# Where a two-block transformer kernel does its modulation steps, frees its last ring blocks and ends its expert stages

## What is computed

```python
# first block, each of two layers
x = x + token_mixer(rms_norm(x, norm_mix[l]), w_in[l], ...)       # two attentions, gates, projections
x = x + peer_ffn(rms_norm(x, norm_ffn[l]), peer_query[l], ...)     # 8 heads x 16 experts of 16384
...
# peer_ffn, for a chunk of 128 tokens
sv, si = lax.top_k(s, PEER_TOPK)                                   # product keys, 2 x 128
act = gelu(einsum('td,thkd->thk', xc, expert_down[eidx]))
out = einsum('thk,thkd->td', g * act, expert_up[eidx])
...
# second block: every layer is modulated by a vector c (and a second stream by c_ctx)
mod = jnp.split(silu(c) @ w_mod[l] + b_mod[l], 6, axis=-1)
p = (rms_norm_2(x, g_norm1[l]) * (1 + scale1) + shift1) @ w_in[l]
x = mixers_and_ffn(x, p, attend_query_blocks(q, k, v), ...)        # attention, Fourier, convolution, pooling, SwiGLU
```

## Time and profile before

| | us |
|---|---|
| median of three runs | 2689.86 |
| lowest and highest | 2688.56, 2691.87 |
| the profiled execution | 2686.94 |
| its span | 2684.9 |
| TensorE matmuls busy | 2498.2 (93% of the span) |
| VectorE, ScalarE, GpSimd busy | 1472.8, 938.3, 595.5 |
| bytes moved by DMA | 817.47 MB, mean 304 GB/s |

### The profile page before, as it was taken

One profiled execution on the slowest core, in us unless ns is written; L12 is line 12 of the kernel. 1 busy time (PEld: TensorE's weight loads), 2 busy tenths in 40 slices (PEclk: granted clock), 3 DMA queues, 4 the chain that ended last, 5 costly groups with the idle time before them and its releaser, 6 DMA issues.

```text
span 2684.9 us, 29496 instructions
## 1 busy us (share of the span) xinstructions
PE 2498.2 (93%) x9800; PEld 1699.9 (63%) x9800; DVE 1472.8 (55%) x3162; ACT 938.3 (35%) x2317; POOL 595.5 (22%) x600
## 2 busy tenths in 40 slices
PE   7999998988888989998998889999889999999999
PEld 6668655533444546677555555567356888868888
DVE  3623576799877637414867776778647200172000
ACT  2351344445544323432444444432446100162000
POOL 0000233333444410001333333333413000030000
PEclk9999899999999999999999999999999999999999
DMA  6574999999999984667999999999972444424444
GB/s 244 176 284 167 370 426 427 427 392 413 404 427 427 420 356 141 250 235 282 413 427 426 427 427 411 421 426 423 423 304 79 148 150 157 159 93 141 148 150 157
DMA packets 113647, 817.47 MB, mean 304 GB/s; under 512 B 12432, under 2 KB 14528, under 8 KB 14944
## 3 DMA queue, kind: packets, MB, share of 16 engines
q0 software_dynamic: 75136, 549.29, 49.1%
q1 hardware_dynamic: 38368, 266.35, 26.8%
HBM read 814.54 MB, written 1.05 MB: 304 GB/s over the span
## 4 chain that ended last, share of the span: by engine, by line
PE 60%; DMA 21%; DVE 11%; issue 4%; ACT 3%; POOL 0%; ACTq 0%; DVEq 0%; SPq 0%; POOLq 0%
PE work L668 43%; DMA arena<-experts,arena 20%; PE acc L668 15%; DVE arena L2001 3%; DVE arena L1790 3%; PE work L760 1%; ACT L1467 1%; DVE small L1790 1%; DMA ring<-stream 1%; ACT arena L1477 1%; POOL arena L631 0%; ACT arena L1469 0%; DVE arena L2239 0%; DMA c<-consts 0%; DVE arena L1949 0%
## 5 line engine op out<-in xcount | busy, mean ns | idle before, releaser
L668 PE MATMUL acc<-arena 128*128 128x512 f32 (+1 forms) x1900 | 888.2, 616 | 124.0 <-ACT arena L1477 121.5
L668 PE MATMUL work<-arena,ring 128*128 128x256 f32 (+2 forms) x3524 | 768.0, 379 | 7.7 <-DMA ring<-stream 2.2
L668 PEld LDWEIGHTS work<-arena,ring 128*128 128x128 f32 x3524 | 667.5, 191 | 112.5 <-issue 17.6
L631 POOL DMA_INDIRECT arena<-experts,arena x512 | 532.3, 1040 | 901.1 <-PE acc L668 720.6
L668 PEld LDWEIGHTS acc<-arena 128*128 128x128 f32 (+1 forms) x1900 | 358.8, 196 | 556.2 <-issue 358.6
L2001 DVE SCALAR_TENSOR_TENSOR arena<-arena,h 128x1024 f32<-128x1024 f32 x256 | 311.9, 1226 | 172.5 <-DMA arena<-experts,arena 169.5
L2001 DVE SCALAR_TENSOR_TENSOR arena<-arena,acc 128x1024 f32<-128x1024 f32 x256 | 308.5, 1220 | 162.1 <-DMA arena<-experts,arena 148.8
L668 PE MATMUL work<-h,ring 128*128 128x256 f32 (+1 forms) x1440 | 329.4, 381 | 8.0 <-DMA ring<-stream 3.8
L668 PEld LDWEIGHTS work<-h,ring 128*128 128x128 f32 x1440 | 268.7, 193 | 76.3 <-issue 37.1
L1467 ACT ACTIVATE arena<-arena 128x2 f32<-128x2 f32 x256 | 52.0, 203 | 608.7 <-DVE arena L2001 404.8
L668 PE MATMUL work<-lent,ring 128*128 128x256 f32 x992 | 224.2, 379 | 0.0
(11 more groups left out here) (263 smaller groups left out, 1834.9 us busy)
## 6 DMA issues: line engine op xcount, KB each, us to landing
ring<-stream SPq DMA_DIRECT2D x252, 1024.0 KB, 5.2
arena<-experts,arena POOLq DMA_INDIRECT x512, 12.5
arena<-na_bias POOLq DMA_DIRECT2D x2, 2048.0 KB, 13.5
arena<-consts POOLq DMA_DIRECT2D x1, 2304.0 KB, 10.9
lent<-consts POOLq DMA_DIRECT2D x2, 1024.0 KB, 7.4
arena<-consts POOLq DMA_DIRECT2D x1, 1816.0 KB, 19.9
x<-x_in SPq DMA_DIRECT2D x1, 1024.0 KB, 5.5
xc<-ctx_in POOLq DMA_DIRECT2D x1, 1024.0 KB, 11.0
```

The source lines that it names most:

```text
L631: pool.indirect_dma_start(rows[:, m % ROWS, :], None, experts[l], bass.IndirectOffsetOnAxis(ap=expert[:, n:n + 1], axis=0))\
L668: ins = nc.tensor.matmul(o, w, r, start=start, stop=stop, **kw)
```

## The change

It moves and counts modulation steps anew, always 24 per layer. Before the norm's sum stand 0 steps in layer 0 and 3 in layer 1 (`MOD_FIRST`); after it 3 in both (1 and 3 before). In layer 1 the units 4, 8 and 12 of the attention have no step. Behind the attention and behind the branch projections stands one step each (2 and 2 before in layer 0, 1 and 1 in layer 1). Of the three steps at the query, one stands before the first score, one behind it and one before the second first-query pass; the first two stand ahead of the query's block in the stream. SP waits for the tokens before it issues the ring. The load of `lent` for layer 1 moves from the end of layer 0 to behind the first projection of layer 1. The four kept ring blocks are released by slots 251 to 254. The last group's two slots are weighed one by one, and the first half of the sums is released by its own semaphore. In layer 1 the last side sum comes before slot 252.

```diff
-MOD_NORM, MOD_TURN, MOD_MERGE, MOD_QUERY = (1, 3), (2, 1), (2, 1), 3
+MOD_FIRST, MOD_NORM = (0, 3), (3, 3)
+MOD_UNITS = [[u for u in range(N_GATE) if l == 0 or u not in (4, 8, 12)] for l in range(DEPTH)]
+MOD_TURN, MOD_MERGE, MOD_QUERY = 1, 1, 3
+MOD_AHEAD = 2
...
             sp.dma_start(x1[:, :, :], x_in.rearrange("k p t -> p k t")).then_inc(sem("x_loaded"), 16)
+            sp.wait_ge(sem("x_loaded"), 16)
...
                 pool.wait_ge(bank_full, ITEMS[f"qk{l}"][0] + 1)
+                pool.dma_start(lent[:, :], consts1[:, C1_FIXED:C1_N]).then_inc(sem("lent_loaded"), 16)
                 if l == 0:
-                    pool.dma_start(lent[:, :], consts1[:, C1_FIXED:C1_N]).then_inc(sem("lent_loaded"), 16)
...
-                if l == 0:
-                    pool.wait_ge(rows_full[m % ROWS], 16 * (m // ROWS + 1))
-                    pool.dma_start(lent[:, :], consts1[:, C1_FIXED:C1_N]).then_inc(sem("lent_loaded"), 16)
-                else:
+                if l:
...
-                            more(1)
+                            more(u)
...
+                mod_steps(MOD_FIRST[l])
+                def mod_beside(u):
+                    if u in MOD_UNITS[l]:
+                        mod_steps(1)
...
                 def slot(n):
-                    if n >= PICKS - 3:
+                    if PICKS - 5 <= n < PICKS - 1:
                         owed.append(kept.pop(0))
...
+                    half_done = sem("half_summed") if n == PICKS - 1 else None
                     for a in range(2):
                         mm(y_acc[t][:, a * 512:(a + 1) * 512], diag[:, at_diag % DIAGS, :], up[:, s, a * 512:(a + 1) * 512],
-                           j == 0, l == 0 and j == SLOTS - 1, inc=rows_free[s] if a else None)
+                           j == 0, j == SLOTS - 1 and (l == 0 or t == TT - 1), inc=rows_free[s] if a else half_done)
...
+                ahead = at[0]
+                at[0] += MOD_AHEAD * BT
+                first_block = at[0] // BT
                 ws = [tile() for _ in range(2 * KD)]
+                behind = at[0]
...
                 first_query_raw()
+                at[0] = ahead
+                mod_steps(1)
                 first_score(0)
+                mod_steps(MOD_AHEAD - 1)
+                at[0] = behind
+                mod_steps(MOD_QUERY - MOD_AHEAD)
                 first_query()
-                read(2 * KD)
-                mod_steps(MOD_QUERY)
+                owed.append(block_free[first_block % RING])
                 mod_turn(2)
...
+                        if l and n == PICKS - 2 * GROUP:
+                            add_side(TT - 1)
...
-                if l:
-                    add_side(TT - 1)
                 for a in range(2):
                     add_up(TT - 1, a)
...
-                    A.need(f"dotted{l}", q + 1)
                     A.need(f"gates{l}", q * GROUP // TOPK + 1)
-                    c = slice(q * GROUP, (q + 1) * GROUP)
+                    if q == GROUPS - 1:
+                        for i in range(GROUP):
+                            A.need(f"dotted{l}", q + i + 1)
+                            weigh_slots(range(q * GROUP + i, q * GROUP + i + 1))
+                    else:
+                        A.need(f"dotted{l}", q + 1)
+                        weigh_slots(range(q * GROUP, (q + 1) * GROUP))
...
                 first_score(0)
+                mod_copy(2)
                 first_query(1)
-                mod_copy(2)
...
                     if l:
                         A.need(f"summed{l}", t + 1)
-                    else:
-                        m = l * PICKS + (t + 1) * SLOTS - 1
+                    if t == TT - 1 and a == 0:
+                        A.need("half_summed", l + 1)
+                    elif l == 0 or t == TT - 1:
                         act.wait_ge(rows_free[m % ROWS], m // ROWS + 1)
```

## The result

| | before | after |
|---|---|---|
| median of the runs on the same chip | 2689.21 | 2666.41 |
| lowest and highest | 2687.29, 2691.87 | 2663.81, 2667.12 |
| the profiled execution, and its span | 2686.94, 2684.9 | 2667.12, 2665.2 |

The ratio of the times is 0.9921, with a 95% interval of 0.9908 to 0.9933: 22.8 us less between the medians, 19.8 us between the two profiled executions. The forecast was 28.1 us less, 2662.

The account below looks back on a forecast made before the run. Bytes bound the two expert stages, TensorE the rest; waits and idle transfers at the joints were to be won. Seven parts, 1.6 + 4.0 + 8.7 + 2.2 + 3.0 + 3.0 + 5.6 = 28.1 us, took 2689.86 to 2662, range 2653 to 2676.

Parts of the forecast that it names:

- (A): Expert stages don't follow their first bytes, so preloading is worth nothing: 16.4 us gained, 2673.5; chance 0.12.
- (C): Entry to block two: TensorE's clock falls to half for over 66 us, making it slower, 2695 or more; chance 0.03.
- Part 1: Start: constants land earlier, first projection starts at 18.7 instead of 20.36; -1.6 us, bounds 0 and -3.
- Part 2: Layer 0, behind the attention: two modulation steps become one, no wait before the branch projections; -4.0 us, bounds -3 and -4.2.
- Part 3: First query, layer 0: steps fill waits, ring blocks load before the gathers, the hole closes; -8.7 us, bounds -4 and -10.
- Part 4: End of layer 0: steps fill the norm's wait, projection starts at 989.3 instead of 992.29; -2.2 us, bounds 0 and -3.5.
- The second term of part 4: End of layer 0: ring data from 969.2 on run beside the last gather, costing 0.8 us at equal shares.
- rival (B): Joints: blocks freed at 251 to 254 delay the last gathers by 2.46 us in each layer; 2670.5; chance 0.10.
- Part 5: Layer 1 gates: units 4, 8 and 12 lose their step of 1.0 us each; -3.0 us, bounds -2 and -3.
- Part 6: Layer 1, first query: ring blocks load before the gathers' data, as in layer 0; -3.0 us, bounds 0 and -5.
- Part 7: End of layer 1: earlier table load, slot 254 and side sum, overlapping halves; -5.6 of a possible -6.2 us, lower bound -3.5.

Follow-up runs that it names:

- the old place of the query's steps: The changed kernel with the three query steps behind first_query again in both layers, and the stream following; measured 2675.05, ratio 0.9953.
- the second execution of the changed kernel: The changed kernel itself run once more without any edit, beside later runs; measured 2665.39, ratio 0.9921 to the kernel before.

## Why the prediction was right, and where it was not

**Its mechanism held**: bytes set the expert stages, and the change wins by filling transfers and TensorE ahead of them. Faster by over 0.2% was right, and 2666.4 lies in the range. (A) is out by the old place of the query's steps, (C) by block two, which takes the same 689.8 us behind its first group. The sum itself was 5.3 us more than the first pair of medians shows, 5.9 more than the second.

**Part 1** was right to 0.1 us in the first projection (18.7 forecast, 18.76), and in its cause: `h` begins to be ready at 17.5 (17.3 forecast), and block 4 lands at 18.63. Part 2 was right in each row (193.3 and one step behind the branch projections). Their sum, -5.6, is -5.4 in the second execution of the changed kernel and -3.6 in the first, where the clock fell in the value projection.

**Part 3**: the ring's blocks before the gathers and the closed hole came as described: the first slot stands 21.5 us behind the first gather, forecast at 21.8 (296.2 less 274.39). At the thirteenth gather 10.0 us were won. The size in the end, -6.3 here and -9.4 among executions with the same fall of the clock, is within its bounds.

**Part 4 is the step that failed.** "The seventh block lands near 989.3": 15.7 us behind the start of the last dot. It landed 17.54 behind it, and the projection started at 17.68. The working dates the issue of the four early blocks, but not that of the three "by the steps". By an estimate from its own numbers, 989.3 comes out if the ring's data run on from 969.2 without a gap (seven blocks, 17.2 us, and 2 to 3 us of the last gather's data between them). In fact there is a gap. The fifth block is issued at 973.02, 2.07 us behind the start of the first step, because its release is taken along by a matmul of the next one; it lands 3.83 us behind the fourth instead of 2.46, and 1.4 of the 2.0 us missed lie there. The seventh, issued at 974.65, lands at 982.82. Eight executions have six steps at this joint and blocks freed by slots 251 to 254 or 247 to 250: in all of them the fifth block is issued 2.1 us behind the first step and the projection starts 11.9 to 12.3 us behind it, however early the first four were freed. So the start of the steps, not the first early block, set the time. The four slots of the ring were used to say which block waits for which, but not to see that they stop the queue until the first step.

The second term of part 4, contention, was sized at 0.8 and is 1.57 in layer 0 (15.75 to 15.84 us to the dot in all eight executions with blocks freed by slots 251 to 254). In layer 1 it is about 1.3: 10.9 and 11.1 us from the last gather's issue to its dot with late blocks, 10.9 in before, and 11.4 to 13.2, 12.2 on average, in ten executions with early ones. Part 4 fell short by 2.7 us in all. The mechanism of rival (B) was there, at 1.6 and 1.3 us per layer instead of 2.5.

**Part 5** (-2.6 for -3.0) was right, but it is not a gain of its own: the kernel without it and without the three steps at the joint takes the same time. **Part 6** came at -2.1 to the last gather's issue for -3.0, less 0.8 for the ring in layer 1, which the sum had charged in layer 0 only. **Part 7** was low by 0.9, and 0.3 beyond the 6.2 that it called possible: the forecast left room for half clock, and it didn't come.

**Sum of the misses.** 28.1 - 2.7 (part 4) - 1.8 (part 6) - 0.4 + 0.9 = 24.1. The profiled execution's 19.8 is that less 2.0 (parts 1 and 2) and 2.4 (part 3), most of which the falls of the clock at 73 us (1.7) and at gather 144 explain. That the range held is no proof of the sum: part 4 and part 6 were too high by 4.5 us together, part 7 too low. The medians, over executions of both sorts, say 22.8 and 22.2.

## What to carry to other kernels

Ask of every prefetch both what it displaces and what it can reach: with four slots in the ring, blocks beyond the fourth start only when the consumer does, so earlier release buys nothing more, while each block put beside the last transfers of a stage costs up to its full length. An edit that fills a gap with work that consumes a scarce buffer is paid back at the next wait for it; test the two halves of such a trade at each joint by itself, as the best mix differed between the layers. Where the last group of a pipeline is split, look for what its first half carries with it, here a table load and TensorE's clock.

## What the runs showed of the hardware

- Same code, same timeline ahead of it, two clocks: at 73 us TensorE was granted half the clock for 3.4 us in four of ten executions. Half clock ahead of a wait for another engine was free (5.29 us of slots, then a wait of 2.21 instead of 3.94), behind the wait it cost about 3.4 us over the next 36 gathers. One profile can so be 2 to 4 us off in a stage without the code having changed.
- Two queues of 1 MB transfers shared the transfer engines one for one: four ring blocks, three of them issued behind the last gather, all landed ahead of it, alternating with the last gathers, and delayed it by 9.96 us, their whole 9.8.
- The load of the constants took 9.2 us beside the tokens and the ring's first blocks, and 6.46 us beside the tokens alone.
